# Expert weights by pairs of neighbouring rows: half as many up transfers, and transposes that read every second column

## The reference, cut to what matters

```python
logits = (xf @ router_w + router_b)
top_val, top_idx = lax.top_k(logits, 4)          # 4 of 32 experts per token
gates = jax.nn.softmax(top_val, axis=-1)
...
hcat = xblk @ w_up[e] + b_up[e]                  # w_up[e]: 1024 x 2048
x_glu = jnp.minimum(hcat[:, :1024], 7.0)
x_lin = jnp.clip(hcat[:, 1024:], -7.0, 7.0)
a = x_glu * jax.nn.sigmoid(1.702 * x_glu) * (x_lin + 1)
y = a @ w_down[e] + b_down[e]                    # w_down[e]: 1024 x 1024
```

## Time and profile before

| | |
|---|---|
| median of 3 runs | 1542.53 us (1540.34 to 1543.96) |
| the profiled execution's own time | 1541.6 us |
| its span in the profile | 1539.5 us |
| mean granted TensorE clock | 0.967 |
| TensorE matmul busy | 1432.4 us |
| VectorE, ScalarE, GpSimd busy | 497.0, 244.4, 12.0 us |
| up transfers | 256 of 1024 KB |
| down transfers | 128 of 1024 KB |
| DMA packets, bytes, mean rate | 95701, 523.72 MB, 340 GB/s |

### The profile page before, as it was taken

How to read it: one execution, slowest core, us unless ns; L and a number is a source line. 1 busy time by engine, 2 the same in 40 slices (tenths; PEclk the granted TensorE clock), 3 DMA queues, 4 the chain that set the end, 5 groups by cost and what they waited for, 6 DMA issues and landing times.

```text
span 1539.5 us, 22212 instructions
## 1 busy us (share of the span) xinstructions
PE 1432.4 (93%) x7709; PEld 587.6 (38%) x7710; DVE 497.0 (32%) x1129; ACT 244.4 (16%) x431; POOL 12.0 (1%) x20
## 2 busy tenths in 40 slices
PE   5999998898867999999999999999999999999993
PEld 1654655555433333333333333333333333323331
DVE  2211354444283222232232222232232232222236
ACT  0001334332010111111111111111111111111110
POOL 0000000000010000000000000000000000000000
PEclk9999999999875999999999999999999999999996
DMA  9958367996663779999999997999999999998940
GB/s 341 373 198 320 121 253 298 357 365 253 209 251 111 302 299 403 419 417 416 418 418 417 417 381 319 400 418 415 418 418 416 417 418 418 415 411 327 401 203 34
DMA packets 95701, 523.72 MB, mean 340 GB/s; under 512 B 10157, under 2 KB 10470, under 8 KB 55483
## 3 DMA queue, kind: packets, MB, share of 16 engines
q1 hardware_dynamic: 92496, 517.62, 84.4%
q0 software_dynamic: 1344, 4.90, 0.9%
q10 hardware_dynamic: 1834, 0.84, 0.2%
HBM read 519.87 MB, written 3.46 MB: 340 GB/s over the span
## 4 chain that ended last, share of the span: by engine, by line
PE 85%; DVE 6%; DMA 4%; issue 2%; SPq 1%; ACT 1%; DVEq 0%; ACTq 0%
PE ps L1573 28%; PE ps L1651 14%; PE ps L1155 7%; PE ps L1517 7%; PE ps L1495 5%; PE ps L1215 5%; PE ps L1417 3%; PE ps L1368 2%; DMA arena<-in_w_in 2%; PE ps L1565 2%; PE ps L1212 2%; PE ps L1445 2%; DMA arena<-in_w_up 2%; PE ps L1583 1%; PE ps L1190 1%
## 5 line engine op out<-in xcount | busy, mean ns | idle before, releaser
L1573 PE MATMUL ps<-arena 128*64 128x512 f32 x2048 | 451.3, 597 | 0.8 <-DMA arena<-in_w_up 0.6
L1573 PEld LDWEIGHTS ps<-arena 128*64 128x64 f32 x2048 | 144.4, 138 | 306.0 <-issue 303.9
L1651 PE MATMUL ps<-arena 128*64 128x512 f32 x1024 | 226.8, 595 | 0.0
L1155 PE MATMUL ps<-arena 128*128 128x128 f32 (+4 forms) x1075 | 153.1, 282 | 50.3 <-DVE arena L819 12.8
L1058 DVE TENSOR_TENSOR arena<-arena,ps 128x512 f32<-128x512 f32 (+1 forms) x198 | 124.4, 680 | 220.6 <-PE ps L1517 215.0
L1155 PEld LDWEIGHTS ps<-arena 128*128 128x128 f32 (+4 forms) x1075 | 116.1, 143 | 124.9 <-issue 81.6
L1102 DVE TENSOR_SCALAR arena<-ps 128x512 f32<-128x512 f32 (+1 forms) x35 | 24.2, 692 | 417.6 <-PE ps L1573 354.7
L1651 PEld LDWEIGHTS ps<-arena 128*64 128x64 f32 x1024 | 70.7, 137 | 152.2 <-issue 152.2
L1517 PE MATMUL ps<-arena 64*128 64x512 f32 x444 | 122.1, 635 | 4.9 <-DVE arena L1082 4.6
L1495 PE MATMUL ps<-arena 128*64 128x512 f32 (+1 forms) x396 | 98.7, 615 | 2.6 <-DVE arena L1046 2.6
L666 ACT ACTIVATE arena<-arena 128x512 f32<-128x512 f32 (+1 forms) x35 | 22.1, 631 | 448.4 <-DVE arena L1102 448.4
(11 more groups left out here) (225 smaller groups left out, 862.9 us busy)
## 6 DMA issues: line engine op xcount, KB each, us to landing
arena<-in_w_up SPq DMA_DIRECT2D x256, 1024.0 KB, 14.8
arena<-in_w_down SPq DMA_DIRECT2D x128, 1024.0 KB, 12.5
arena<-in_w_ada SPq DMA_DIRECT2D x12, 2048.0 KB, 17.4
arena<-in_cache_k SPq DMA_DIRECT2D x16, 1536.0 KB, 8.8
arena<-in_cache_v SPq DMA_DIRECT2D x16, 1536.0 KB, 8.9
arena<-in_w_in SPq DMA_DIRECT2D x6, 2048.0 KB, 20.6
arena<-in_cache_k SPq DMA_DIRECT2D x32, 192.0 KB, 4.3
arena<-in_cache_v SPq DMA_DIRECT2D x32, 192.0 KB, 9.6
```

Source lines behind the costliest of these rows:

```text
L1155: return nc.tensor.transpose(o, i, ident[0:n, 0:n])
L1573: ins = mm(bank(part)[64 * h:64 * h + 64], xe_t[:, 0, at:at + 64], up_w[:, k, FF * part + 512 * h:FF * part + 512 * h + 512], start=False, ...
L1651: ins = mm(bank(3)[64 * h:64 * h + 64], a_t[:, 0, at:at + 64], dn_w[:, kk, 512 * h:512 * h + 512], start=kk == 0, stop=kk == KC - 1)
```

## The change

Both weights are seen as `(m p k) n` with k = 2: partition p of block m holds rows 256m + 2p and 256m + 2p + 1, which are neighbours in memory. The up weights come in four transfers of 2 MiB with four semaphores; SyncE waits until both chunks of a pair are used, and TensorE waits before the first chunk of a pair. The down weights come in four transfers as before, with other rows on the partitions. Chunk 2m + j now holds the rows 256m + 2p + j, so `turn_gathered` and `turn_act` read every second column (`pairs(c)`), and the matmuls stay as they are.

```diff
--- before.py
+++ after.py
@@ -240,8 +240,8 @@
         wada_d = t["w_ada"][0].rearrange("(k p) n -> p k n", p=128)
         win_d = t["w_in"][0].rearrange("(k p) n -> p k n", p=128)
         wo_d = t["w_o"][0].rearrange("(k p) n -> p k n", p=128)
-        wup_d = t["w_up"][0].rearrange("e (k p) n -> e k p n", p=128)
-        wdn_d = t["w_down"][0].rearrange("e (m k p) n -> e m p k n", p=128, k=2)
+        wup_d = t["w_up"][0].rearrange("e (m p k) n -> e m p k n", p=128, k=2)
+        wdn_d = t["w_down"][0].rearrange("e (m p k) n -> e m p k n", p=128, k=2)
         ck = t["cache_k"][0].rearrange("b s h e -> b s (h e)")
         cv = t["cache_v"][0].rearrange("b s h e -> b s (h e)")
 
@@ -251,7 +251,7 @@
         ada_used, ada_late, hot_in, k_high_in, v_in, wo_in = map(
             sem, ("ada_used", "ada_late", "hot_in", "k_high_in", "v_in", "wo_in"))
         k_low_in = [sem(f"k_low_in{half}") for half in range(2)]
-        up_in = [sem(f"up_in{k}") for k in range(KC)]
+        up_in = [sem(f"up_in{m}") for m in range(KC // 2)]
         dn_in = [sem(f"dn_in{m}") for m in range(KC // 2)]
         bup_in, bup_used, up_used, dn_used = map(sem, ("bup_in", "bup_used", "up_used", "dn_used"))
         const_in, c_in, rows_in, bada_in, bada_late, x_ready, tabc_in = map(
@@ -436,8 +436,8 @@
                 src = vectors[1 + b:2 + b, 0:3 * D].to_broadcast([NS, 3 * D]).rearrange("p (a b) -> p a b", a=3)
                 sp.dma_start(mod_s[NS * b:NS * b + NS], src).then_inc(mod_late, 16)
             sp.dma_start(x1[0:64, 2, :], t["x_sample"].rearrange("b s d -> (b s) d")).then_inc(mod_late, 16)
-            for k in range(KC):
-                sp.dma_start(up_w[:, k, :], wup_d[0, k]).then_inc(up_in[k], 16)
+            for m in range(KC // 2):
+                sp.dma_start(up_w[:, 2 * m:2 * m + 2, :], wup_d[0, m]).then_inc(up_in[m], 16)
             for m in range(KC // 2):
                 if m == 1:
                     sp.wait_ge(u2_ready, 3)
@@ -448,10 +448,10 @@
             with sp.Fori(1, items) as i:
                 e = i % NE
                 load_expert(e, i)
-                for k in range(KC):
-                    sp.wait_ge(up_used, (i - 1) * KC + k + 1)
-                    sp.dma_start(up_w[:, k, :], wup_d[bass.ds(e, 1), k].rearrange("o p n -> (o p) n")
-                                 ).then_inc(up_in[k], 16)
+                for m in range(KC // 2):
+                    sp.wait_ge(up_used, (i - 1) * KC + 2 * m + 2)
+                    sp.dma_start(up_w[:, 2 * m:2 * m + 2, :], wup_d[bass.ds(e, 1), m].rearrange(
+                        "o p k n -> (o p) k n")).then_inc(up_in[m], 16)
                 for m in range(KC // 2):
                     sp.wait_ge(dn_used, (i - 1) * (KC // 2) + m + 1)
                     sp.dma_start(dn_w[:, 2 * m:2 * m + 2, :], wdn_d[bass.ds(e, 1), m].rearrange(
@@ -1488,6 +1488,10 @@
             ins.then_inc(gt_done, 1)
 
 
+            def pairs(c):
+
+                return slice(256 * (c // 2) + c % 2, 256 * (c // 2) + 256, 2)
+
             def gather(blocks):
 
                 for tt, (_, n) in enumerate(TILES):
@@ -1507,7 +1511,7 @@
                 pe.wait_ge(xn_ready, turn_no)
                 for v in range(blocks):
                     for c in range(2 if v else 4):
-                        ins = turn(bank(1 + 2 * v, 128 * c, 128 * c + 128), xe_nat[:, v, 128 * c:128 * c + 128], 128)
+                        ins = turn(bank(1 + 2 * v, 128 * c, 128 * c + 128), xe_nat[:, v, pairs(c)], 128)
                 ins.then_inc(gathered_turned_done, 1)
 
             def scatter(tt, banks, blocks, more=False):
@@ -1593,7 +1597,8 @@
                     ins.then_inc(bup_used, 1)
                     for k4 in range(0, KC, 4):
                         for k in range(k4, k4 + 4):
-                            pe.wait_ge(up_in[k], i * 16 + 16)
+                            if k % 2 == 0:
+                                pe.wait_ge(up_in[k // 2], i * 16 + 16)
                             ins = up_main(k)
                             if blocks == 1:
                                 ins.then_inc(up_used, 1)
@@ -1616,7 +1621,7 @@
                 def turn_act(v):
                     p = 64 if v else 128
                     for c in range(4):
-                        ins = turn(bank(2 * v, p * c, p * c + p), act_l[0:p, v, 128 * c:128 * c + 128], p)
+                        ins = turn(bank(2 * v, p * c, p * c + p), act_l[0:p, v, pairs(c)], p)
                     ins.then_inc(at_done[v], 1)
 
                 def add_up(tt, blocks):
```

## The result

The changed kernel is slower: 1549.4 us (median of 5 runs, 1546.7 to 1551.6) against 1541.9 (5 runs on the same chip), a ratio of 1.0046 with a 95% interval of 1.0035 to 1.0058. The forecast was 1541.9 and no difference that can be measured.

A forecast was written before the change was run, and what follows sets the result against it. TensorE was taken to bound the expert loop. The profiled 1541.6 us less a 0.6 us wait gave 1541.0; with the runs' median 0.9 above the profiled execution, the forecast was 1541.9 us, range 1538.8 to 1546.5.

The forecast's parts named there:

- What bounds the kernel: Expert loop: TensorE bounds it at 29.41 us a plain pass; slower transfers queue up, causing one wait of 0.6 us.
- the wait: TensorE's up matmuls near 1348 us: one wait of 0.6 us on an expert's up weights, forecast to go.
- DMA packets: Weight transfers: neighbouring rows travel as one packet, saving 0.8 us per expert; queue grows 0.65 us a pass, not 1.44.
- Coarser chunks: Up transfers of 2 MiB: allowance falls from 27.5 to 25.8 us, queue reaches 21.4 at worst; the 0.6 us wait goes.
- the 1.74 us of the start: Up-weight queue: extra 1.74 us at worst at a stretch's start, if the DMA engines had run dry.
- SyncE's queue: SyncE's waits and issues: four fewer of each per expert, 0.33 us each; no time gained on TensorE.
- Turns over every second column: Weight loads of eight turns a pass: reading with a step of two was taken to cost nothing.
- the bounds, 0 to 0.106 us a turn: Turns' weight loads: from free to half speed; the half-speed rival meant 0.85 us a pass, 1572 us, chance 0.08.
- the 0.012 us that would decide: Stepped turns: price per turn from which the loss reaches the measurable 3.1 us (3.1 / 256).
- The clock: TensorE's clock staying low for longer: named as a way to be wrong, without a price or chance.

The follow-up runs named there:

- coarse-only kernel: Kernel before with four up transfers of 2 MiB and their waits, but the old rows on each partition and plain turns; ratio 1.0001.
- kernel with a step of four: Kernel before with its transposes reading every fourth column (gathered overflow rows every second), weights in their old order; ratio 1.0053.
- the turns alone: Kernel before with only its two transposes reading every second column, weights in their old order; ratio 1.0028, medians 1548.6 and 1543.2 us.
- kernel with seven stepped turns: Kernel before with transposes reading every second column, less one of turn_act's four in each pass; ratio 1.0015.
- ninth plain turn: Kernel before with the last transpose of turn_act(0) done twice in each pass, without a step; ratio 1.0043, and 1.0028 when run again.
- changed kernel with seven turns: Changed kernel less one of turn_act's four transposes in each pass; ratio 1.0015.

## Why the prediction was wrong, step by step

- **What bounds the kernel** held. TensorE's pieces of a pass make the time, and all but the turns are found again to 0.01 us. Transfers quicker by 0.55 us an expert brought nothing but the wait.
- **DMA packets** held in kind: the neighbours travel as one packet, 3788 in 100 us. The saving was put at 0.8 us per expert; the pass of 29.54 plus a growth of 0.76 makes 30.30 against 30.85, so it was 0.55.
- **Coarser chunks** held: no wait on up weights. The end of the queue was forecast at 21.4 of 25.8 us and came to 19.7. It began at 12.2 in place of 14.9, for the most part because the 1.74 us of the start were not due (in the coarse-only kernel it began at 13.8, not 15.3), and grew by 0.76 in place of 0.65.
- **SyncE's queue** cost nothing, as forecast.
- **Turns over every second column** is the step that failed: "I take nothing". Of the bounds, 0 to 0.106 us a turn, the value was 0.016 on average, and eight turns in 32 passes make 4.1 us. Working with one price per turn was itself too simple: about 10 ns for each turn, which is under the 0.012 us that would decide, and some 50 ns more for the head of the group. The reason given was that a stepped load spans no more memory per ns than the moving operand reads. The kernel with a step of four contradicts the argument itself: it spans twice as much and costs the same. The prediction had even worked out that 0.012 us a turn would decide the sign, and then chose between the two ends by a comparison that said nothing about the small values between them. Of the two halves of the rule in the Trainium skill ("SBUF — State Buffer", section "Door 1: The DMA port swizzle"), a step of two fp32 should be free by the first; it was not. By the second each crossing to a new line pays; a step of four crosses twice as many lines as a step of two, and eight turns took 0.01 us more. Neither half gives what these loads show.
- **The clock** was no term of the sum, and only named as something unpriced. A spell costs 1.6 to 1.7 us. Seven profiles of kernels with their turns as before show 1, 1, 2, 2, 2, 2 and 2 of them after the first expert; seven with stepped turns 3, 3, 4, 4, 4, 5 and 6; three with plain turns added 2, 4 and 5. On average that is 1.7 against 4.1, or 4 us. The whole of the runs gives less. By the ratios the turns alone lost 4.3 us and the changed kernel 7.1, twice; by the medians side by side 5.3, and 7.5 and 5.6. The mean granted clock of nearly every run is on record: 0.9669 over 181 runs of kernels with their turns as before, 0.9656 over 65 with stepped turns, 0.9660 over the 11 of the changed kernel. A spell of 1.6 us in 1545 lowers that mean by 0.001, so by this estimate stepped turns bring about one spell more, 1 to 2 us, and not 2.4. It is a rough one, because the mean also holds the part ahead of the loop, where the clock is low for longer and differs from run to run: the kernel with seven stepped turns has three spells in the loop, and its profiled execution is the fastest of its 12, at 1540.0 us.
- **Open:** what brings the spells. The two kernels with seven stepped turns (three and six spells at 29.42 and 29.43 us) speak against the length of the pass alone, and the ninth plain turn (five) against stepped loads alone; but each rests on one or two profiles, of a number that varied between two and five for the same kernel. All lie in an overflow pass or in the pass beside it (once the one ahead, in the changed kernel with seven turns), and every one of these edits also touches those passes. A kernel that changes the turns of the overflow passes only was not run. How much of the 7.5 us the spells make is therefore not settled: 1 to 2 us by the recorded clocks, about 3 as what the stepped loads leave over.

## What to carry to other kernels

Where an engine is busy without a gap, work out the price per instruction that would decide the sign before choosing between far bounds. Here it was 0.012 us, a tenth of the upper bound, and the nearest row could not exclude it. Price the first of a group by itself: here it cost five times as much as each of the others. Put a change of order where an engine has time: the same interleaving was free in ScalarE's and VectorE's copies, and in 64-column weight loads among 512-column matmuls, and cost 4 us in front of short transposes. A faster transfer under a bound TensorE buys slack only.

## What the runs showed of the hardware that was not expected

- A step in the weight load made the first of eight fp32 transposes 56 ns longer (384 for 328) and spaced the others 117 to 122 ns apart in place of 109; with every fourth column in place of every second it was 0.01 us more for eight.
- A 128-column fp32 weight load with a step took 207 ns (step two) and 210 ns (step four) as recorded, against 140 for neighbours; a 64-column load under long matmuls took 138 against 137.
- Packets of 16 and 8 KB, in place of 8 and 4, brought the loop from 418 to 424 GB/s.
- TensorE was at its lower clock level for short spells, 1.6 to 1.7 us lost in each, in and beside the overflow passes, where its matmuls wait for VectorE (up to 1.6 us at a time), in some executions and not in others: the same kernel with nine plain turns showed two spells and five.
